# Slots of the weight ring named by hand, parts of the S5 mixer split inside its scan, and the hand-over at every seam cut into halves

## Time and profile before

| | us |
|---|---|
| median of 3 runs | 1542.59 |
| lowest, highest | 1538.04, 1546.05 |
| the profiled execution, own time | 1546.46 |
| its span, first to last instruction | 1544.7 |
| TensorE matmuls busy | 1290.9 (84%) |
| VectorE, ACT, POOL busy | 683.5, 445.7, 297.7 |
| mean granted clock of TensorE | 0.874 |

### The profile page before, as it was taken

One profiled execution on the slowest core, in us unless ns is written; L12 is line 12 of the kernel. 1 busy time (PEld: TensorE's weight loads), 2 busy tenths in 40 slices (PEclk: granted clock), 3 DMA queues, 4 the chain that ended last, 5 costly groups with the idle time before them and its releaser, 6 DMA issues. The chain is left out here.

```text
span 1544.7 us, 22095 instructions
## 1 busy us (share of the span) xinstructions
PE 1290.9 (84%) x8942; PEld 930.3 (60%) x8942; DVE 683.5 (44%) x1085; ACT 445.7 (29%) x659; POOL 297.7 (19%) x293
## 2 busy tenths in 40 slices
PE   6989586898878887876996668999959988799996
PEld 3547363333333343334865657999949667699995
DVE  1454752222212211215244646767653273477675
ACT  2223122111111111113343314444433431344442
POOL 0000564633033032032211610000024410000000
PEclk9999687888898888986998787999979967799998
DMA  9563473999999999996773113554424301244541
GB/s 375 220 257 109 157 306 139 428 429 429 428 428 428 429 428 429 429 428 255 295 305 111 63 74 114 200 192 175 190 109 164 136 1 40 96 179 188 189 178 41
DMA packets 35999, 369.62 MB, mean 239 GB/s; under 512 B 4069, under 2 KB 5614, under 8 KB 12270
## 3 DMA queue, kind: packets, MB, share of 16 engines
q1 hardware_dynamic: 33552, 364.66, 58.4%
q10 hardware_dynamic: 2398, 4.27, 0.8%
HBM read 367.84 MB, written 1.06 MB: 239 GB/s over the span
## 5 line engine op out<-in xcount | busy, mean ns | idle before, releaser
L598 PE MATMUL ps<-W_parts 128*128 128x256 f32 (+1 forms) x2672 | 388.5, 309 | 3.6 <-DVE W_parts L2191 2.0
L598 PEld LDWEIGHTS ps<-W_parts 128*128 128x128 f32 x2672 | 363.2, 194 | 29.4 <-issue 4.5
L598 PE MATMUL ps<-ring,W 128*32 128x512 f32 x1536 | 223.2, 730 | 71.7 <-DMA ring<-in_w_up 42.0
L598 PE MATMUL ps<-W 128*32 128x64 f32 (+6 forms) x1696 | 168.2, 312 | 23.9 <-DVE W L2132 8.8
L598 PEld LDWEIGHTS ps<-ring,W 128*32 128x32 f32 x1536 | 51.2, 127 | 222.5 <-issue 136.8
L449 POOL TENSOR_TENSOR ring_parts<-ring,ring_parts 128x2048 fp32r<-128x2048 f32 x18 | 98.5, 5482 | 374.5 <-ACT ring_parts L441 374.5
L598 PEld LDWEIGHTS ps<-W 128*32 128x32 f32 (+3 forms) x1696 | 112.6, 175 | 86.2 <-issue 76.1
L598 PE MATMUL ps<-XH_parts,ring_parts 128*128 128x256 f32 x512 | 99.0, 296 | 24.2 <-DVE W_parts L2137 15.2
L2159 DVE TENSOR_TENSOR W_parts<-ring,W_parts 128x2048 fp32r<-128x2048 f32 x44 | 100.8, 2292 | 28.6 <-ACT W_parts L1420 28.5
L598 PEld LDWEIGHTS ps<-XH_parts,ring_parts 128*128 128x128 f32 x512 | 85.1, 204 | 25.2 <-issue 22.4
L2045 DVE COPY W<-ps 128x1024 f32<-128x1024 f32 x16 | 19.6, 1225 | 175.3 <-PE ps L598 175.3
(11 more groups left out here) (342 smaller groups left out, 1548.4 us busy)
## 6 DMA issues: line engine op xcount, KB each, us to landing
ring<-in_w_gate SPq DMA_DIRECT2D x32, 2048.0 KB, 21.7
ring<-in_w_up SPq DMA_DIRECT2D x32, 2048.0 KB, 26.6
ring<-in_w_down SPq DMA_DIRECT2D x32, 2048.0 KB, 22.6
ring<-in_ada_w SPq DMA_DIRECT2D x24, 2048.0 KB, 9.9
ring<-in_up SPq DMA_DIRECT2D x44, 1024.0 KB, 5.5
ring<-in_dn SPq DMA_DIRECT2D x44, 512.0 KB, 3.5
ring<-in_fox_in SPq DMA_DIRECT2D x6, 2048.0 KB, 7.7
ring<-in_w_in SPq DMA_DIRECT2D x2, 2048.0 KB, 14.0
```

The lines of the kernel that those rows point to most:

```text
L598: return pe.matmul(o, l, r, start=a, stop=z_, skip_group_check=True, **kw)
```

## The change

- `weight_plan` takes a slot by name (`to`). The twelve adaLN blocks of the scan take slots 4, 5, 0, 1, 2, 3, 4, 5, then 2, 3, then 2, 3; w_glu's blocks go to slots 0/1 and 4/5 between them, w_out's to 2/3 and 0/1, the first ffn's to 4, 5 and 2, 3, the fox blocks from 4/5 on. So the first adaLN block of the scan waits for the first half of the u product, the next two for its second half; w_glu 0 waits for adaLN products 3 and 4 of the scan, w_glu 1 for 7 and 8; fox 0 waits for the last up product of the first ffn, and fox 1, which is free earlier, stands behind it in the queue.
- Every `root` first takes the root of one column (`warm`), ahead of its wait.
- XN is signalled in two halves of 512 columns; `turn` transposes the first four feature blocks when the first halves are there.
- In the split, ACT copies the high part of features 4 to 7 as well, and VectorE makes the low part of features 0 to 3 first. TensorE's first product begins with four of its eight blocks and waits for the rest in its middle.
- In the scan: y's first half is split (ACT behind the Gelu of turn 4, VectorE behind turn 5), w_glu 0's high part is copied behind the Gelu of turn 4 and its low part made by POOL behind `kx(6)`; w_glu 1's behind the Gelu of turn 6 and `kx(7)`. The gate rows stand before the last `far`. Buffers move so that this is free (tu, yl, y2h, y2l).
- POOL begins the low part of S5's w_in only behind the squares of seam 3, and that of w_out's block 4 only behind y's low part.
- The ffn opens its banks before it waits, makes the gate rows behind the first `up`, and closes each bank behind its last product.
- Semaphores are merged (bst/cst to st_ready, decay/kx to near_ready, o_var and o_std to the qkv ones, f_abs/F_ready to F_parts; the copy of Bt waits for table_mm in place of bt_mm; VectorE's own waits in the scan go through its chain of marks). Not shown below.

```diff
-    def load(name, n=1, times=1, apart=False):
+    def load(name, n=1, times=1, apart=False, to=None):
         nonlocal at
+        at = at if to is None else to
...
-    load("ada", ADA_STEPS - ADA_FIRST)
-    load("s5", 4, apart=True)
-    load("up0", 2, NF // 2)
-    load("down0", 2, NF // 2)
+    load("ada", 8, to=4)
+    load("s5", 1, apart=True, to=0)
+    load("ada", 2, to=2)
+    load("s5", 1, apart=True, to=4)
+    load("ada", 2, to=2)
+    load("s5", 1, apart=True, to=2)
+    load("s5", 1, apart=True, to=0)
+    load("up0", 2, NF // 2, to=4)
+    load("down0", 2, NF // 2, to=2)
...
-        tu = XNf[:, 0:1024].rearrange("p (s k q j) -> p s k q j", s=2, k=2, q=4)
+        tu = O_[:, 0:1024].rearrange("p (s k q j) -> p s k q j", s=2, k=2, q=4)
...
-        s5l, yl, y2h, y2l = low_at(S5_LOW), low_at(0), low_at(NC * T), low_at(2 * NC * T)
+        s5l, yl, y2h, y2l = low_at(S5_LOW), low_at(5 * D), low_at(0), low_at(2 * D)
...
-                    pe.wait_ge(S("xn_normed"), k + 1 - (k > 6))
+                    pe.wait_ge(S("xn_first"), k + 1 - (k > 6))
                     if k != 1:
-                        pe.wait_ge(S("xn_normed1"), {0: 1, 7: 6}.get(k, k))
+                        pe.wait_ge(S("xn_first1"), {0: 1, 7: 6}.get(k, k))
                 for c in range(NC):
+                    if c == NC // 2 and k != 6:
+
+                        pe.wait_ge(S("xn_normed"), k + 1 - (k > 6))
+                        if k != 1:
+                            pe.wait_ge(S("xn_normed1"), {0: 1, 7: 6}.get(k, k))
...
+            def first_ready(k):
+
+                pe.wait_ge(S("ht_act"), k + 1)
+                pe.wait_ge(S("ht_low0"), SPLIT_TURNS.index(k) + 1)
+
+            def second_ready(k):
+
                 pe.wait_ge(S("ht_dve"), k + 1)
...
+                        if turned is not None and t == 0 and c == NC // 2:
+                            second_ready(turned)
...
+                if ct == NC - 1:
+
+                    pe.wait_ge(S("mod_ready"), 1)
+                    pe.wait_ge(S("ada_kept"), ADA_STEPS)
+                    gate_rows(0, (6, 7))
                 far(ct)
...
                 turn(turned)
-                ht_ready(turned)
-                gate_rows(2 * k + 1, (2, 3))
                 for b in range(4, 8):
...
+                            if first and a == 0 and c == NC // 2:
+                                second_ready(turned)
...
+                            if closing and n + t < 2:
+                                closed(4 + 2 * n + t)
                     last.then_inc(S("down_mm"), 1)
-
-                up(0, 0)
+                    if closing:
+                        closed(7)
+
+                def closed(b):
+
+                    mm(ps[:, b, :], zb[0:1, 0:P], zb[0:1, :], False, True).then_inc(S("ffn_mm"), 1)
+
+                first_ready(turned)
+                up(0, 0, True)
+                gate_rows(2 * k + 1, (2, 3))
...
-                down(NF // 2 - 1, 1)
-                for b in range(4, 8):
-                    mm(ps[:, b, :], zb[0:1, 0:P], zb[0:1, :], False, True).then_inc(S("ffn_mm"), 1)
+                down(NF // 2 - 1, 1, True)
...
+                own(act.activation(warm[:, :], ident[:, 0:1], ACT.Sqrt))
                 act.wait_ge(S(before), value)
...
-                    act.activation(XN[:, 1, :], X[:, 1, :], ACT.Copy, scale=rs[:, 1:2]
-                                   ).then_inc(S("xn_normed1"), 1)
+                    for half, done in ((0, "xn_first1"), (1, "xn_normed1")):
+                        a = slice(half * BANK, half * BANK + BANK)
+                        act.activation(XN[:, 1, a], X[:, 1, a], ACT.Copy, scale=rs[:, 1:2]).then_inc(S(done), 1)
...
                     last = act.activation(split[0][:, 0:4, :], HT[:, 0:4, :], ACT.Copy)
                 last.then_inc(S("ht_act"), 1)
+                if split:
+
+                    act.wait_ge(S("ht_wide"), SPLIT_TURNS.index(k) + 1)
+                    act.activation(split[0][:, 4:8, :], HT[:, 4:8, :], ACT.Copy).then_inc(S("ht_high"), 1)
...
-                    act.wait_ge(S("bt_mm"), i + 1)
+                    act.wait_ge(S("table_mm"), i + 1)
...
             apart_high(act, 0)
@@ -1390,18 +1434,17 @@
                                ).then_inc(S("y_copied"), 1)
                 if ct + 2 < NC:
                     cst(ct + 2)
-            for n in (2, 3):
-                apart_high(act, n)
+                if ct == 4:
+                    act.activation(XNr[:, 0:4, :], HT[:, 0:4, :], ACT.Copy).then_inc(S("y_high"), 1)
+                if ct in (4, 6):
+                    apart_high(act, 2 + (ct - 4) // 2)
+            act.wait_ge(S("y_copied"), NC)
+            act.activation(XNr[:, 4:8, :], HT[:, 4:8, :], ACT.Copy).then_inc(S("y_high"), 1)
+            apart_high(act, 4)
             act.wait_ge(S("gate_mm"), 1)
-            act.wait_ge(S("rot_out"), NC)
             act.activation(GBs.rearrange("p (b n) -> p b n", b=2), ps[:, 6:8, :], ACT.Copy
                            ).then_inc(S("gate_copied"), 1)
-            act.wait_ge(S("y_copied"), NC)
-            for j in range(2):
-                act.activation(XNr[:, 4 * j:4 * j + 4, :], HT[:, 4 * j:4 * j + 4, :], ACT.Copy
-                               ).then_inc(S("y_high"), 1)
-            apart_high(act, 4)
             for j in range(4):
                 if j == 2:
                     apart_high(act, 5)
...
+            pool.wait_ge(S("squares0"), 3)
             apart_low(pool, 0, 1)
             apart_low(pool, 1, 1)
...
             for ct in range(NC):
                 decay(ct)
                 kx(ct)
-
-            for n in (2, 3):
-                for half in range(2):
-                    apart_low(pool, n, half)
+                if ct >= 6:
+                    for half in range(2):
+                        apart_low(pool, ct - 4, half)
+            pool.wait_ge(S("y_low"), 2)
             for n in (4, 5):
                 apart_low(pool, n, 1)
...
-                ts(XN[:, 0, :], X[:, 0, :], rs[:, 0:1], None, ALU.mult).then_inc(S("xn_normed"), 1)
+                for half, done in ((0, "xn_first"), (1, "xn_normed")):
+                    a = slice(half * BANK, half * BANK + BANK)
+                    ts(XN[:, 0, a], X[:, 0, a], rs[:, 0:1], None, ALU.mult).then_inc(S(done), 1)
...
                 if split:
-                    own(last)
+                    last.then_inc(S("ht_wide"), 1)
                     high, low = split
-                    own(v.tensor_copy(high[:, 4:8, :], HT[:, 4:8, :]))
-                    tt(low[:, 4:8, :], HT[:, 4:8, :], high[:, 4:8, :].bitcast(F32), ALU.subtract)
                     v.wait_ge(S("ht_act"), k + 1)
-                    last = tt(low[:, 0:4, :], HT[:, 0:4, :], high[:, 0:4, :].bitcast(F32), ALU.subtract)
+                    tt(low[:, 0:4, :], HT[:, 0:4, :], high[:, 0:4, :].bitcast(F32), ALU.subtract
+                       ).then_inc(S("ht_low0"), 1)
+                    v.wait_ge(S("ht_high"), SPLIT_TURNS.index(k) + 1)
+                    last = tt(low[:, 4:8, :], HT[:, 4:8, :], high[:, 4:8, :].bitcast(F32), ALU.subtract)
                 last.then_inc(S("ht_dve"), 1)
...
             for half in range(2):
                 for t in range(NT):
                     o = XN[:, t, BANK * half:BANK * half + BANK]
                     last = ts(o, o, ss13[:, 0, 2 * half + t:2 * half + t + 1], None, ALU.mult)
-            last.then_inc(S("xn_normed"), 1)
+                last.then_inc(S(("xn_first", "xn_normed")[half]), 1)
...
+            def y_low(j):
+
+                v.wait_ge(S("y_high"), j + 1)
+                a = slice(4 * j, 4 * j + 4)
+                tt(yl[:, a, :], HT[:, a, :], XNr[:, a, :].bitcast(F32), ALU.subtract).then_inc(S("y_low"), 1)
...
-                v.wait_ge(S("turned_back"), ct + 1)
+                    ready = driven(ct + 1)
+                own.wait(back)
                 if ct >= 2:
                     v.wait_ge(S("cy_mm"), ct - 1)
                 tt(xst[:, b, :, 0, 1:TJ + 1], to[:, 0, 0], to[:, 1, 1], ALU.subtract)
                 tt(xst[:, b, :, 1, 1:TJ + 1], to[:, 0, 1], to[:, 1, 0], ALU.add).then_inc(S("rot_out"), 1)
+                if ct == 5:
+                    y_low(0)
             modulation(ADA_STEPS, 1, LAYERS)
-            for j in range(2):
-                v.wait_ge(S("y_high"), j + 1)
-                a = slice(4 * j, 4 * j + 4)
-                tt(yl[:, a, :], HT[:, a, :], XNr[:, a, :].bitcast(F32), ALU.subtract).then_inc(S("y_low"), 1)
+            y_low(1)
```

More of the change, by code:

```diff
@@ L1067, in up, with down @@
                     last.then_inc(S("up_mm"), 1)
-                def down(i, b):
+                def down(i, b, closing=False):
                     pe.wait_ge(S("down_low"), i * 2 + (NF * k + b + 1))
@@ L1343, in cst @@
                                           ACT.Copy)
-                last.then_inc(S("cst_ready"), 1)
+                last.then_inc(S("st_ready"), 1)
             def bst(ct):
@@ L2124, in _ @@
```

(6 more changed lines are left out.)

73 lines of the change are left out of this document (37 added, 36 removed).

## The result

The changed kernel takes **1513.63 us**, the median of four runs (1509.63 to 1514.89), against 1540.96 us for four runs of the kernel before on the same chip (1538.04 to 1546.05). The ratio is 0.9826, with a 95% interval of 0.9805 to 0.9847. The forecast was 1514.1 us in a range of 1501 to 1527. The profiled execution is one of 1513.65 us, so it stands at the median; against the profiled execution of before (1546.46) it is 32.8 us shorter, where the sum said 28.5.

What follows compares the result with a forecast made beforehand. TensorE, busy 84% of the span, was taken to wait for the experts' transfer stream and at the seams. Terms summing to 28.5 us gave 1518.0 from the profiled 1546.46, 1514.1 from the median; range 1501 to 1527.

Steps and rivals of the forecast that it cites:

- part 1: Root: table load ahead of the wait saves 1.0 us where ACT idles, nothing behind w_o; XN's half signal 0.55 a passage.
- part 3: Start gains 1.4 us, w_o 2.2, the second root loses 0.1; these 3.5 us carry through the experts.
- Part 4: Behind the experts: holding POOL back gains 0, the split of features 1.9 us; bounds 0 and 3.9.
- Part 2: Split of the features: TensorE starts 1.9 us earlier in each of six passages, 1.5 in turn 6.
- Part 5: Scan's end: 14.2 us gained, less 8.1 for POOL-VectorE collision, 1.0 low clock, 0.5 loads; net 4.6, bounds 0 and 14.2.
- Rival (a): The scan escapes the POOL-VectorE collision: 8.1 + 1 us more gained, 1505 us; chance 0.25.
- Part 6: Slots: the scan's adaLN loads, no longer prefetched, are just fast enough; costs 0.5 us, bounds 0 and 3.
- Rival (d): Slower: adaLN loads without a prefetch bound the scan, 62 us more, near 1576 us; chance 0.02.
- Part 7: Into both ffns: zero matmuls in idle time, gate rows later; second up product 5.2 us earlier each, bounds 4.1 and 5.9.
- Part 8: Out of the ffns: closing each bank behind its last product lets VectorE start adding about 2.1 us sooner.
- Part 9: Into fox: XN comes 1.6 us earlier, with the split of features 3.5; bounds 1 and 6.
- Part 10: Turn 6 gains 1.5 us; the end 3.1, from closing 2.1 and root 1.0; Bt's copy 0.

Runs made afterwards that it cites:

- experiment 4: Changed kernel without the dummy Sqrt ahead of the roots; 1515.54 us.
- experiment 6: Changed kernel with the features split as before: VectorE makes its own copy and both low halves before TensorE starts; 1523.65 us.
- experiment 3: Changed kernel with, behind the experts and ahead of fox, the dummy Sqrt before ACT's weight copy and POOL's subtraction waiting for XN; 1509.42 us.
- experiment 5: Changed kernel with the four banks closed after the last down product of each ffn, as before; 1519.18 us.
- experiment 7: Changed kernel with gate matmuls, then zero matmuls, between the finished features and the first up product in both ffns, as before; 1518.06 us.
- experiment 10: Changed kernel with ACT and VectorE taking up the second w_out block behind the last glu tile, not amid the tiles; 1499.22 us.
- experiment 9: Kernel of experiment 8 with the last two adaLN loads in slots 4 and 5, issued ahead of glu block 1; 1501.71 us.
- experiment 2: Changed kernel with POOL splitting glu block 0 one turn later, just ahead of block 1; 1510.27 us.
- experiment 1: Changed kernel with glu block 0 split by VectorE in turn 6, leaving POOL only block 1; 1506.06 us.
- experiment 8: Changed kernel with VectorE splitting glu block 0 over turns 5 and 6, POOL waiting for XN, dummy Sqrt dropped at two roots and moved ahead of fox; 1505.57 us.
- experiment 11: Kernel of experiment 8 with the edits of experiment 9 and experiment 10 both added; 1490.99 us.

## Why the prediction was right

**The time** is within 0.5 us of the forecast, better than the working deserves: against the profiled execution the sum is 4.3 short, and the profile of before stands 3.9 above the median that was given. That these two nearly cancel is luck.

**Parts 1, 3 and 4** held in the main: 1.0 us at each clear root (experiment 4), XN behind the experts held up by ACT and then by POOL for 3.11 us. The half signal of XN gives 0.4 us where 0.55 was taken: from the scaling's start to the turn 0.87 us, 1.29 before. What part 1 called "nothing" behind w_o is a loss of 0.7 us by the dummy (part 3 had the whole root at -0.1), and behind the experts it costs 1.0. Into w_o 3.0 us had come by the first product where 3.6 were due, because the adaLN product in front took 3.10 us and, not the features, ended last.

**Part 2** is the second largest and the surest: 1.80 us in each of three passages, 1.2 at w_o, and 1.25 to 1.5 in the ffns (experiment 6).

**Part 5**, the largest, was right in its mechanism. TensorE goes on 3.9 us behind the scan's last product where it took 20.0 (2.1 of them the gate rows, which now stand inside the scan); no run takes the splits inside the scan back, so this is read from the timelines alone. The price is the collision. A turn, from one far product to the next, takes 11.1 us when nothing disturbs it. Seven profiles hold this scan unchanged (the changed kernel and experiments 3 to 7 and 10):

| kernel | adaLN wait | VectorE's pair takes | turn with the collision | turn behind it | scan, us |
|---|---|---|---|---|---|
| changed | 0.55 | 8.55 | 19.0 | 13.8 | 99.4 |
| 4 | 0.41 and 0.55 | 8.66 | 19.0 | 10.8 | 96.5 |
| 5 | 2.42 | 6.66 | 19.3 | 13.7 | 96.8 |
| 3 | 2.35 | 4.77 | 19.3 | 12.6 | 96.4 |
| 6 | 2.64 | 3.24 | 19.2 | 11.8 | 94.4 |
| 10 | 3.08 | 4.89 | 19.2 | 10.9 | 92.8 |
| 7 | 2.86 | 5.07 | 19.2 | 10.8 | 92.7 |

Where TensorE waits long for a load, VectorE's products come later and find less of POOL's piece left. But in all seven the far product starts 2.0 to 2.6 us behind the end of that piece, and the turn is 7.9 to 8.1 us too long. So the collision and the load's wait don't add, as the 8.1 and 0.5 of the sum do: they stand in for one another, and together cost some 8. Rival (a), no collision, came in none of them. With the load in time and the split moved to VectorE that turn takes 14.0 us and the scan 88.1 (experiment 9); what the collision alone costs, with the load in time, no run shows.

The scan's length scatters for another reason, the clock in the other turns. The turn behind the collision in the changed kernel and in experiment 7 (TensorE's busy time, granted clock, DMA share, GB/s):

```profile
825.73:839.48 13.75, 9.70 (x144) 0.50 0.01 2
```

```profile
829.17:839.99 10.82, 6.78 (x144) 0.82 0.33 137
```

That turn took 10.8 us in the kernel before, so the forecast's "about 1 us" of low clock was 0 to 3. Why the clock came back sooner in some executions is open. The net gain in the profiled execution is 4.5 us (6.3 to 10.8), forecast 4.6; with the shortest of the seven scans in its place it would be some 11. So the mechanism was foreseen, and the closeness of the number is luck.

**Part 6** took 0.5 us with bounds 0 and 3. The profiled execution has 0.55, and five of the other six 2.3 to 3.1: the upper bound is the usual case, and TensorE's waiting for adaLN loads was one of the prediction's own signs of being wrong. The loads themselves came as it had them. From 762 to 815 us they land 4.9 us apart, and the last one 67.1 us after the scan's start, for 64 and 5 in the sum. What fell short was to compare only the last load with the last product. The last but one, thirteenth in the queue, lands 62.0 to 62.5 us after the scan's start in all ten profiles with this order, and an undisturbed TensorE wants it at 59.4. In the changed kernel's profile TensorE came 2.3 us late by itself, after two stretches of low clock, and so waited only 0.55. Experiment 9 has this adaLN load one place further up; it lands at 57.4, and the wait is gone. Rival (d) had the right mechanism at a small size.

**Parts 7 and 8** held: 4.9 us came from the first w_out product to the third tile of the first ffn (5.2 forecast), of which the order of the gate rows is 2.9 (experiment 7); closing gives 2.1 at the end and 2.0 into fox (experiment 5).

**Parts 9 and 10** are where the sum is short. Fox came as forecast. But from its first product to turn 7 the changed kernel gains 5.9 us, and the sum had 3.1 (1.5 for turn 6, and 1.0 and 0.55 for the root ahead of turn 7). Of the 5.9, turn 6 to turn 7 gives 3.8: 1.8 from the split, as measured in experiment 6; 1.4 more up to the first product, because the 16 transposes ran in 1.97 us in place of 3.67, at the high clock; 1.4 from the root, less 0.8 for the products between. The other 2.1 come in the fox attention, which the change hardly touches and for which the sum had nothing; its last 47 to 49 us had a mean clock of 0.70 against 0.64. That stretch took 137.9 us before, 135.8 in the changed kernel and 132.4 to 136.5 in the eleven experiments. The clock alone doesn't explain it: experiment 10 took 135.4 with 0.62 at its end. Why it is shorter wasn't tried, and stays open.

**What no part spoke of** is the wait ahead of the w_out products, 10.55 us before and 10.73 after. The change leaves it alone, and so did I. In the changed kernel it is the dearest single wait, and moving two instructions takes 8.1 us of it (experiment 10).

## What to carry to other kernels

Look at what a piece of filler work on POOL does to the instructions of VectorE that have two SBUF inputs, and give such work to the engine that idles in that turn, in pieces that fit its gap. On ACT or VectorE never put work that waits for a load ahead of the last links of a chain that TensorE waits for. When the DMA engines are full, the order of the queue is the schedule: compare every load in it with its product, not only the last, and issue last what is needed last (experiment 9). And measure such a stretch turn by turn, in several profiles: the same scan took 92.7 to 99.4 us, while the turn in question took 19.0 to 19.3.

## What the runs showed of the hardware that I had not expected

With two instructions queued on each of VectorE and POOL, the two alternated in all four profiles that have the case (the changed kernel, experiments 2, 4 and 5): the second product, due when the first ended, waited through another whole subtraction (4.98 us), as it came behind it. It was all or nothing: a scaling issued 0.05 us ahead of POOL's start took 0.17 us (experiment 4), one issued 1.4 us behind it 3.11. And idle time costs again in the products behind it, but not by a fixed amount: the w_out products took 23.8 to 25.2 us behind 10.5 to 10.8 us of idle (the kernel before, the changed one and experiments 1 to 9), and 22.66 and 24.08 (experiments 10 and 11) behind 2.6.
